# Samples' delta rule on TensorE: states streamed past w and q, and state updates on two row groups

## The chip, the cores and the metric

The kernel runs on one core of one Trainium2 chip. The time is that of one whole execution on the device in microseconds (us), as the median of several runs. Engines: TensorE (PE; its weight loads are listed as PEld), VectorE (DVE), ScalarE (ACT), GpSimd (POOL), and SyncE (SP), which issues most DMAs.

## The reference

A decoder trunk of two layers takes one step for a prompt of 512 tokens and for 8 samples of 8 new tokens each. In each layer one input projection feeds three mixers in parallel: a linear recurrence (RG-LRU), sparse attention (NSA), and the gated delta rule. Their outputs are gated, projected, merged and added to the residual. All is float32.

The change concerns the delta rule of the samples. It has 4 heads and, for each sample b and head h, a state S of 128x128. With a chunk's u, w, q, k (after decay), the reference's step is

```python
def step(S, xs):
    u_, w_, qk_, qdec_, kdec_, gl_ = xs
    vn = u_ - jnp.einsum('bhcd,bhde->bhce', w_, S)
    o = jnp.einsum('bhcd,bhde->bhce', qdec_, S) + jnp.einsum('bhce,bhef->bhcf', qk_, vn)
    S = gl_[..., None, None] * S + jnp.einsum('bhcd,bhce->bhde', kdec_, vn)
    return S, o
```

For the samples one chunk holds a sample's 8 tokens, so each of the 32 states is multiplied with 8 rows of w and 8 of q, and updated once. Outputs are o (normed and gated further on) and the new states.

## The kernel before

Activations lie channels on partitions, tokens along the free axis: 576 tokens (512 + 64), in halves of 288. All work is written out once per layer for each engine; each engine runs its own list in order, and counting semaphores join them.

**The dense stream.** TensorE's projections are cut into units (UNITS), each of 4 or 8 dense steps; a step is one matmul of 128x128 stationary with 288 columns (mm at L935), in the trace two records. A unit goes to PSUM bank u % 2 and is evicted by DVE or ACT; TensorE waits, before unit u, for the eviction of unit u-2. Two chunks of channels form a pair of seven units, named "1", "6", "2", "7", "5", "4", "3" in this order (PRODUCTS), of 4 steps each: a product scheme with sums of activations and of weights. Units "1" and "2" are evicted by ACT, the others by DVE. At the eviction of a "5", DVE also forms the three weight sums of the next pair (weight_sums: three operations on 128x512, L1804, L1801, L1804), for which it first waits until that pair's slot of the weight ring has landed; at that of a "6" it forms a fourth. The ring has two slots (RING). From L1226 on the order of pairs is: the last pair of z gates of the delta rule, then the merge gates ("mg") of branch 0, where each pair is followed by four units "ow" (output projection) of 4 steps. ACT turns the gates of "5", "4" and "3" of a merge pair into tanh when it comes to the unit two further on.

**What sets the order.** Between TensorE's small steps stand fills: fill(n, end) issues the next n dense steps, up to unit `end`. Each small step calls step(name), which records how many dense units were complete at that place. take_before(name, count), in DVE's and ACT's lists, evicts all the units recorded there before the engine waits for that step. So the count of dense steps ahead of a small step decides which evictions stand ahead of its consumer. The fills here end at unit U_MG2 at the latest (in attention 7 units later).

**The delta rule of the samples** (last entry of DN_GROUPS), by TensorE's lines:
- L1216/L1217: u and w, turned, to banks 6 and 7 (f_mm). The fill of 4 steps behind it is unit "5" of the last z pair. DVE copies uT (L2165), ACT wT (L1670).
- L1226, 32 matmuls: the state S0[:, b, h] is stationary (128x128), 16 columns stream past it, 8 of w and 8 of q of one sample. Step b_pe 1. DVE subtracts (L2168, helper line L1804), b_vt.
- turns of vn (helper line L864), b_pe 2; DVE copies vn (L2172), b_vn; L1239, products within the chunk, b_pe 3; DVE adds to q (L2178, L2179), b_so. ACT, which waits for b_so, squares it (L1688).
- for each head h, L1248: two matmuls of 512 columns, 64 tokens contracted. The moving operand bvm is vn of this head repeated 8 times under a mask of samples (bmask), made by DVE (L2186, helper line L1798, 64x1024), b_vm. Steps b_pe 4 to 7. DVE adds the result (two banks, 128x1024) to the states (L2193, helper line L1801), b_sn. Before each add, DVE takes the evictions recorded at that head's step.
- POOL decays the states in place (L824) behind b_pe 1, four operations.

After the loop TensorE waits for the fourth b_sn, then fills 2 steps and goes on with the sums of squares (L968, on column groups of 32, for the norms "o", "k", "q") and six broadcasts of the roots (L981, on row groups of 32), each followed by a product on DVE (L1981); then the keys are turned (L864). ACT waits for the fourth b_sn too, and forms logarithms (L1575), roots (L1582) and SiLU (L1706).

**SP's list.** After weights(19), the slot of merge pair 0, SP waits for the fourth b_vm (L684), then issues two loads of constants (L685: 858 KB, L686: 576 KB, into places that the delta rule used till then) and only then weights(20), the slot of merge pair 1 (L619, 1024 KB).

The end of DVE's loop over the heads (from L2181 on):

```python
                for h in range(DN_H + 1):
                    ...
                    if h >= 1:
                        g = h - 1
                        dve.wait_ge(s["b_gl"], past["b_gl"] + h)
                        take_before("b_pe", 3 + h)
                        dve.wait_ge(s["b_pe"], past["b_pe"] + 3 + h)
                        ...
```

## Time and profile before

| | |
|---|---|
| median of 3 runs | 1883.47 us (1881.01 to 1885.6) |
| the profiled execution | span 1882.8 us; no other time of it is given |
| TensorE busy | 1816.3 us, 96% |
| VectorE, ScalarE, GpSimd busy | 964.6, 516.7, 91.5 us |
| mean granted TensorE clock | 0.994 |
| DMA | 170.08 MB, mean 90 GB/s |

In a row of the timeline or of the chain the first number is the start in us from the span's start, the second the length in us; then come engine, line, operation, tiles, shapes and the number of records (x). A float32 matmul has two records. Square brackets give the time that the engine stood idle before it, and what ended that. DVE's operations are made by helpers, so that L1798 is any multiply, L1801 any add, L1804 any subtract, and L864 any turn; the shape tells which one it is. The granted clock is a share of 2.4 GHz.

### The profile page before, as it was taken

What the parts mean: (1) busy time and instruction counts of PE and PEld (TensorE: products, weight loads), DVE (VectorE), ACT (ScalarE), POOL (GpSimd) and SP (SyncE); (2) the same over time, 40 slices, a digit from 0 to 9 for tenths busy, and PEclk for the clock granted to TensorE, in tenths of its full rate; (3) what the DMA queues carried; (4) which work ended last, traced back from release to release, by engine and by line L of the source; (5) the groups of instructions that cost most, each with busy time, mean ns of one, the idle gap of its engine ahead of it and who ended that gap; (6) DMA issues with size and microseconds to landing.
All of it is one profiled execution on the core that took longest, in us unless ns stands there. A gap on an engine that the chain in (4) does not pass through costs nothing.

```text
span 1882.8 us, 29564 instructions
## 1 busy us (share of the span) xinstructions
PE 1816.3 (96%) x11454; PEld 1301.3 (69%) x11454; DVE 964.6 (51%) x2246; ACT 516.7 (27%) x1161; POOL 91.5 (5%) x133
## 2 busy tenths in 40 slices
PE   7999999999899999999999999999999999999999
PEld 5777688886665577676467777888856555776763
DVE  2749554534765555533137585545347565554321
ACT  3142313013356612200112433020142565221100
POOL 0000201001200000000000002010012000000000
PEclk9999999998999999999999999999999999999999
DMA  6312402023341135645042142021144311464411
GB/s 214 97 46 70 113 26 45 24 62 102 114 134 34 31 110 159 182 138 161 0 161 83 52 100 62 24 46 55 31 132 130 88 34 34 133 190 127 157 73 39
DMA packets 196529, 170.08 MB, mean 90 GB/s; under 512 B 49248, under 2 KB 186898, under 8 KB 195942
## 3 DMA queue, kind: packets, MB, share of 16 engines
q1 hardware_dynamic: 192164, 150.11, 27.4%
q0 software_dynamic: 4064, 18.03, 3.0%
q8 instruction: 91, 1.49, 0.3%
q14 instruction: 48, 0.39, 0.1%
q10 hardware_dynamic: 162, 0.05, 0.0%
HBM read 153.67 MB, written 21.71 MB: 93 GB/s over the span
## 4 chain that ended last, share of the span: by engine, by line
PE 81%; DVE 11%; issue 3%; SPq 2%; ACT 2%; DMA 1%; ACTq 0%; DVEq 0%
PE PS L935 53%; PE PS L864 6%; DVE arena L1873 3%; PE PS L1307 2%; PE PS L1320 2%; PE PS L1155 2%; PE PS L1137 1%; PE PS L1157 1%; DVE arena L1798 1%; PE PS L1376 1%; SPq L652 1%; PE PS L1226 1%; PE PS L1041 1%; PE PS L1248 1%; PE PS L1169 1%
## 5 line engine op out<-in xcount | busy, mean ns | idle before, releaser
L935 PE MATMUL PS<-hT,ring 128*128 128x288 f32 x2464 | 655.1, 411 | 7.5 <-DVE arena L2082 3.7
L935 PEld LDWEIGHTS PS<-hT,ring 128*128 128x128 f32 x2464 | 456.3, 191 | 138.7 <-issue 11.7
L935 PE MATMUL PS<-tt,ws 128*128 128x288 f32 x736 | 207.3, 414 | 13.4 <-DVE sg L1931 4.4
L935 PE MATMUL PS<-zs,owr 128*128 128x288 f32 x768 | 208.3, 413 | 6.8 <-DVE sg L1804 4.2
L935 PEld LDWEIGHTS PS<-zs,owr 128*128 128x128 f32 x768 | 140.0, 192 | 50.3 <-issue 12.8
L935 PEld LDWEIGHTS PS<-tt,ws 128*128 128x128 f32 x736 | 132.7, 190 | 57.6 <-issue 9.4
L864 PE MATMUL PS<-con,arena 128*128 128x128 f32 (+5 forms) x934 | 144.6, 281 | 14.4 <-DMA arena<-in_nsa_k_norm 10.3
L864 PEld LDWEIGHTS PS<-con,arena 128*128 128x128 f32 (+5 forms) x934 | 107.7, 140 | 72.8 <-issue 42.2
L1801 DVE TENSOR_TENSOR sg<-PS,sg 128x288 f32<-128x288 f32 x140 | 64.0, 457 | 139.7 <-PE PS L935 138.4
L935 PE MATMUL PS<-arena 128*128 128x512 f32 (+1 forms) x320 | 124.8, 594 | 2.1 <-DVE sg L1931 2.1
L935 PE MATMUL PS<-tt,ring 128*128 128x288 f32 x368 | 107.5, 426 | 0.0
L1873 DVE SCALAR_TENSOR_TENSOR arena<-arena,par 128x512 f32<-128x512 f32 x192 | 99.4, 518 | 6.3
L935 PEld LDWEIGHTS PS<-arena 128*128 128x128 f32 (+1 forms) x320 | 52.8, 180 | 71.0 <-issue 68.0
L1557 ACT ACTIVATE sg<-PS 128x288 f32<-128x288 f32 x46 | 18.5, 403 | 260.1 <-PE PS L935 259.9
L1731 ACT ACTIVATE arena<-PS,sm 128x128 f32<-128x128 f32 (+3 forms) x128 | 66.8, 523 | 70.8 <-DVE sm L2282 64.9
L935 PEld LDWEIGHTS PS<-tt,ring 128*128 128x128 f32 x368 | 69.1, 197 | 20.9 <-issue 3.0
L2282 DVE CUSTOM_DVE_ANT_0 PS<-PS,con 128x128 f32<-128x128 f32 (+3 forms) x128 | 61.8, 505 | 41.1 <-PE PS L1307 41.1
L1804 DVE TENSOR_TENSOR arena<-arena,PS 128x512 f32<-128x512 f32 (+3 forms) x70 | 43.4, 622 | 56.0 <-PE PS L1157 36.7
L1722 ACT ACTIVATE arena<-arena,sm 128x128 f32<-128x128 f32 (+3 forms) x128 | 64.7, 553 | 23.3 <-DVE sm L1798 23.3
L1798 DVE TENSOR_TENSOR arena<-arena 128x2304 f32<-128x2304 f32 (+3 forms) x24 | 39.7, 1655 | 58.1 <-ACT arena L1612 22.2
L1962 DVE SCALAR_TENSOR_TENSOR arena<-PS,arena 128x512 f32<-128x512 f32 x18 | 12.5, 692 | 103.9 <-PE PS L935 97.2
L1804 DVE TENSOR_TENSOR ws<-ring 128x512 f32<-128x512 f32 x92 | 63.5, 690 | 3.3 <-DMA ring<-in_w_in 1.7
(306 smaller groups left out, 2123.6 us busy)
## 6 DMA issues: line engine op xcount, KB each, us to landing
ring<-in_w_in SPq DMA_DIRECT2D x54, 1024.0 KB, 5.4
arena<-in_cache_nsa_kv SPq DMA_DIRECT2D x128, 192.0 KB, 2.7
ring<-in_w_in SPq DMA_DIRECT2D x32, 256.0 KB, 4.6
arena<-in_state_nsa_win SPq DMA_DIRECT2D x32, 256.0 KB, 3.4
arena<-in_cache_nsa_kv SPq DMA_DIRECT2D x128, 64.0 KB, 1.8
arena<-in_w_out SPq DMA_DIRECT2D x4, 2048.0 KB, 8.3
out_win_sample<-in_state_nsa_win POOLq DMA_DIRECT2D x2, 4032.0 KB, 23.1
arena<-in_x_prompt SPq DMA_DIRECT2D x8, 512.0 KB, 5.5
```

Source lines behind the costliest of these rows:

```text
L864: return nc.tensor.transpose(dst, src, ident[0:src.shape[0], 0:src.shape[0]])
L935: ins = mm(to, w, x, start=start, stop=stop, skip_group_check=True)
L1155: mm(new[0][m], Y[m, h, m], blocks(w[m], sz, 0), start=True, stop=True)
L1307: mm(PS[:, 4 + g, 0:q0 + P], qk7[m, r, q0:q0 + P], qk7[m, 5 + br, 0:q0 + P], start=True, stop=True).then_inc(s["a_s"], 1)
L1320: ins = mm(PS[g * HD:(g + 1) * HD, 7, rp * 2 * P:(rp + 1) * 2 * P], ktok[:, kb, col:col + HD], pTring[j % 2][:, g * 2 * P:(g + 1) * 2 * P] ...
L1722: A(p, p, ACT.Copy, scale=sm8[:, 7, u % 8:u % 8 + 1]).then_inc(s["a_n"], 1)
L1731: A(pring[slot % PRING][:, 0:width], PS[:, 4 + slot % 2, 0:width], ACT.Exp, scale=-1.0, bias=sm8[:, 0, k:k + 1], accum_out=sm8[:, 1, k:k + ...
L1798: return V.tensor_tensor(dst, a, b, ALU.mult)
L1801: return V.tensor_tensor(dst, a, b, ALU.add)
L1804: return V.tensor_tensor(dst, a, b, ALU.subtract)
L1873: ins = stt(out=d, in0=e, scalar=w(j), in1=d, op0=ALU.mult, op1=ALU.add)
L2282: V.tensor_tensor_reduce(out=raw, in0=raw, in1=C("causal")[:, 3 * P - q0:4 * P], scale=-1.0, scalar=-NEG, op0=ALU.add, op1=ALU.min, accum_ ...
```

## The change

The states become the moving operand. For each head and each pair j of samples, 32 stationary columns (8 of w and 8 of q of both samples) stand in column group j, and the two states of the pair stream past them, 256 columns; each sample's own rows come out token-first, with the other sample's beside them, unused. ACT and DVE copy the two result banks to SBUF (swq), eight turns bring them back channels-first in banks 6 and 7, and DVE takes from these the w part (two subtractions) and the q part (two copies). A fill of 6 steps stands between the products and the turns. DVE lays q beside w first (f_v 5). Between w products and vn's turns there is thus one b_pe step more. The state update of each head contracts 32 tokens (4 samples) on each of two row groups, with a mask of 4 columns, so that bvm is 64x512 instead of 64x1024, and each of the two matmuls gives four samples.

```diff
@@ -69,7 +69,7 @@
-    ("U", P), ("R", P), ("Um", P), ("Us", P), ("Rs", P), ("Ums", P), ("lev", 7 * P), ("bmask", DEC_BATCH),
+    ("U", P), ("R", P), ("Um", P), ("Us", P), ("Rs", P), ("Ums", P), ("lev", 7 * P), ("bmask", DEC_BATCH // 2),
@@ -124,7 +124,7 @@
-    c["bmask"] = np.arange(DEC_BATCH)[None, :] == row // DEC_SEQ
+    c["bmask"] = np.arange(DEC_BATCH // 2)[None, :] == row // DEC_SEQ % (DEC_BATCH // 2)
@@ -333,8 +333,8 @@
-    i_wm=31, i_x=31, i_xm=31, f_mm=5, f_u=4, f_v=4, f_w=5, m_mm=3, u_mm=4, f_m=3, q_w=3, q_s=4, q_n=3, q_oe=4, b_gl=4,
-    b_pe=7, b_so=1, b_vt=1, b_vn=1, b_vm=4, b_sn=4, dn_ok=1, mg_ok=32, small_in=96, sm_in=32, ln_ok=5, sum_ok=97,
+    i_wm=31, i_x=31, i_xm=31, f_mm=5, f_u=4, f_v=6, f_w=6, m_mm=3, u_mm=4, f_m=3, q_w=3, q_s=4, q_n=3, q_oe=4, b_gl=4,
+    b_pe=8, b_so=1, b_vt=1, b_vn=1, b_vm=4, b_sn=4, dn_ok=1, mg_ok=32, small_in=96, sm_in=32, ln_ok=5, sum_ok=97,
@@ -468,16 +468,28 @@
         uT, vnT = (arena[:, at + k * DN_H * T_S:at + (k + 1) * DN_H * T_S].rearrange("p (h n) -> p h n", h=DN_H)
                    for k in range(2))
         vn = tmp["B"][0:T_S, 1]
-        wT0, dc0 = A_DN["Sb"][0], A_DN["c"][0]
-        wT = arena[:, wT0:wT0 + DN_H * T_S].rearrange("p (h n) -> p h n", h=DN_H)
-        def w_and_q(h, b):
-
-            a, q = wT0 + h * T_S + b * DEC_SEQ, dc0 + h * T + SEQ + b * DEC_SEQ
-            return arena[:, a:a + 2 * (q - a)].rearrange("p (x c) -> p x c", x=2)[:, :, 0:DEC_SEQ]
+        wq = area(A_DN, "Sb").rearrange("p (h j x u) -> p h j x u", h=DN_H, j=4, x=2)
+        def w_and_q(h, j):
+            return area(A_DN, "Sb")[:, (4 * h + j) * 32:(4 * h + j) * 32 + 32]
+        def by_pairs(ap):
+            return ap.rearrange("p h (j u) -> p h j u", j=4)
         S0 = area(A_DN, "S0").rearrange("p (b h e) -> p b h e", b=DEC_BATCH, h=DN_H)
         rowd = area(A_DN, "rowd")[0:27]
-        bvm = [area(A_DN, "kbv")[:, k * 1024:(k + 1) * 1024] for k in range(2)]
+        bvm = [area(A_DN, "kbv")[:, k * 512:(k + 1) * 512] for k in range(2)]
+        swq = area(A_DN, "kbv")[:, 1024:2048]
+        def from_state(i, x):
+            return PS[:, 6 + i, :].rearrange("p (h j x u) -> p h j x u", h=DN_H, j=4, x=2)[:, :, :, x, i * DEC_SEQ:(i + 1) * DEC_SEQ]
+        def of_pairs(ap, i):
+            return ap.rearrange("p h (j i t) -> p h j i t", i=2, t=DEC_SEQ)[:, :, :, i]
         def diagonal(n):
@@ -1220,11 +1232,20 @@
                         fill(4, u0 + U_MG2)
                         pe.wait_ge(s["f_w"], past["f_w"] + k + 1)
                         pe.wait_ge(s["s0_in"], past["s0_in"] + 16 * DEC_BATCH)
+                        pe.wait_ge(s["f_v"], past["f_v"] + 5)
                         for h in range(DN_H):
-                            for b in range(DEC_BATCH):
-                                at = h * P + b * 2 * DEC_SEQ
-                                ins = mm(PS[:, 3, at:at + 2 * DEC_SEQ].rearrange("p (x t) -> p x t", x=2), S0[:, b, h, :],
-                                         w_and_q(h, b), start=True, stop=False, skip_group_check=True)
+                            for j in range(4):
+                                dst = PS[32 * j:32 * j + 32, 4 + h // 2, h % 2 * 2 * P:(h % 2 + 1) * 2 * P]
+                                ins = mm(dst.rearrange("p (i e) -> p i e", i=2), w_and_q(h, j), S0[:, 2 * j:2 * j + 2, h, :],
+                                         start=True, stop=True, skip_group_check=True)
+                        step("b_pe")
+                        ins.then_inc(s["b_pe"], 1)
+                        fill(6, u0 + U_MG2)
+                        pe.wait_ge(s["f_w"], past["f_w"] + 6)
+                        pe.wait_ge(s["f_v"], past["f_v"] + 6)
+                        for i in range(2):
+                            for h in range(DN_H):
+                                ins = turn(PS[:, 6 + i, h * P:(h + 1) * P], swq[:, (2 * h + i) * P:(2 * h + i + 1) * P])
                         step("b_pe")
                         ins.then_inc(s["b_pe"], 1)
                         fill(4, u0 + U_MG2)
@@ -1245,8 +1266,8 @@
-                                ins = mm(PS[:, 4 + 2 * (h % 2) + c, :], kq[0:T_S, 0, h, 0:P],
-                                         bvm[h % 2][0:T_S, c * 512:(c + 1) * 512], start=True, stop=True)
+                                m = slice(32 * c, 32 * c + 32)
+                                ins = mm(PS[:, 4 + 2 * (h % 2) + c, :], kq[m, 0, h, 0:P], bvm[h % 2][m], start=True, stop=True)
@@ -1667,8 +1688,11 @@
                     if TILES[group[0]][0] >= SEQ:
                         take_before("f_mm", NTILE)
                         act.wait_ge(s["f_mm"], past["f_mm"] + NTILE)
-                        A(wT, bank4(7, T_S), ACT.Copy).then_inc(s["f_w"], 1)
-                        take_before("b_pe", 3)
+                        A(wq[:, :, :, 0], by_pairs(bank4(7, T_S)), ACT.Copy).then_inc(s["f_w"], 1)
+                        take_before("b_pe", 1)
+                        act.wait_ge(s["b_pe"], past["b_pe"] + 1)
+                        A(swq[:, 0:512], PS[:, 4, :], ACT.Copy).then_inc(s["f_w"], 1)
+                        take_before("b_pe", 4)
                         act.wait_ge(s["b_so"], past["b_so"] + 1)
                         break
                     for li, k in enumerate(group):
@@ -1686,7 +1710,7 @@
                 for n in range(DN_H):
                     A(dc[:, 4 + n], dc[:, n], ACT.Square).then_inc(s["sq_ok"], 1)
-                take_before("b_pe", 3 + DN_H)
+                take_before("b_pe", 4 + DN_H)
                 act.wait_ge(s["pv"], taken(u0 + U_NZ, "V"))
                 act.wait_ge(s["pa"], taken(u0 + U_NZ, "A"))
                 act.wait_ge(s["b_sn"], past["b_sn"] + DN_H)
@@ -2162,34 +2186,39 @@
                 take_before("f_mm", NTILE)
                 dve.wait_ge(s["f_mm"], past["f_mm"] + NTILE)
+                V.tensor_copy(wq[:, :, :, 1], by_pairs(dc[:, 0:4, SEQ:T])).then_inc(s["f_v"], 1)
                 link(V.tensor_copy(uT, bank4(6, T_S)))
                 take_before("b_pe", 1)
                 dve.wait_ge(s["b_pe"], past["b_pe"] + 1)
-                sub(vnT.rearrange("p h (b t) -> p h b t", t=DEC_SEQ), uT.rearrange("p h (b t) -> p h b t", t=DEC_SEQ),
-                    PS[:, 3, :].rearrange("p (h b x t) -> p h b x t", h=DN_H, x=2, t=DEC_SEQ)[:, :, :, 0]).then_inc(s["b_vt"], 1)
+                V.tensor_copy(swq[:, 512:1024], PS[:, 5, :]).then_inc(s["f_v"], 1)
                 take_before("b_pe", 2)
                 dve.wait_ge(s["b_pe"], past["b_pe"] + 2)
-                V.tensor_copy(vn, bank4(2, P, T_S)).then_inc(s["b_vn"], 1)
+                q_s = dc[:, 0:4, SEQ:T]
+                for i in range(2):
+                    ins = sub(of_pairs(vnT, i), of_pairs(uT, i), from_state(i, 0))
+                ins.then_inc(s["b_vt"], 1)
+                for i in range(2):
+                    ins = V.tensor_copy(of_pairs(q_s, i), from_state(i, 1))
+                link(ins)
                 take_before("b_pe", 3)
                 dve.wait_ge(s["b_pe"], past["b_pe"] + 3)
-                from_s = PS[:, 3, :].rearrange("p (h b x t) -> p h b x t", h=DN_H, x=2, t=DEC_SEQ)[:, :, :, 1]
-                within = PS[:, 2, 0:DN_H * T_S].rearrange("p (h b t) -> p h b t", h=DN_H, t=DEC_SEQ)
-                q_s = dc[:, 0:4, SEQ:T].rearrange("p h (b t) -> p h b t", t=DEC_SEQ)
-                link(V.tensor_copy(q_s, from_s))
-                add(q_s, q_s, within).then_inc(s["b_so"], 1)
+                V.tensor_copy(vn, bank4(2, P, T_S)).then_inc(s["b_vn"], 1)
+                take_before("b_pe", 4)
+                dve.wait_ge(s["b_pe"], past["b_pe"] + 4)
+                add(q_s, q_s, PS[:, 2, 0:DN_H * T_S].rearrange("p (h n) -> p h n", h=DN_H)).then_inc(s["b_so"], 1)
                 dve.wait_ge(s["b_vn"], past["b_vn"] + 1)
                 for h in range(DN_H + 1):
                     if h < DN_H:
                         if h >= 2:
-                            take_before("b_pe", 3 + h - 1)
-                            dve.wait_ge(s["b_pe"], past["b_pe"] + 3 + h - 1)
-                        mul(bvm[h % 2][0:T_S].rearrange("p (b e) -> p b e", b=DEC_BATCH),
-                            rep(vn[:, h, :], DEC_BATCH), bc(C("bmask")[0:T_S], P)).then_inc(s["b_vm"], 1)
+                            take_before("b_pe", 4 + h - 1)
+                            dve.wait_ge(s["b_pe"], past["b_pe"] + 4 + h - 1)
+                        mul(bvm[h % 2][0:T_S].rearrange("p (b e) -> p b e", b=DEC_BATCH // 2),
+                            rep(vn[:, h, :], DEC_BATCH // 2), bc(C("bmask")[0:T_S], P)).then_inc(s["b_vm"], 1)
                     if h >= 1:
                         g = h - 1
                         dve.wait_ge(s["b_gl"], past["b_gl"] + h)
-                        take_before("b_pe", 3 + h)
-                        dve.wait_ge(s["b_pe"], past["b_pe"] + 3 + h)
+                        take_before("b_pe", 4 + h)
+                        dve.wait_ge(s["b_pe"], past["b_pe"] + 4 + h)
                         add(S0[:, :, g], S0[:, :, g],
                             PS[:, 4 + 2 * (g % 2):6 + 2 * (g % 2), :].rearrange("p a (b e) -> p (a b) e", e=P))\
                             .then_inc(s["b_sn"], 1)
```

## Rows read from the trace of the kernel before

**Rows 1.** The page, part 4: shares of the chain that ended last.

```profile
PE 81%; DVE 11%; issue 3%; SPq 2%; ACT 2%; DMA 1%; ACTq 0%; DVEq 0%
```

**Rows 2.** The chain in order of time, layer 0: start, us, what.

```profile
282.87 1.94 PE PS L935 x8
...
424.40 9.28 PE PS L1226 x64
433.68 4.03 PE PS L935 x8
...
440.84 1.03 PE PS L1239 x8
...
444.01 1.94 PE PS L1248 x4
...
448.09 1.91 PE PS L1248 x4
450.00 2.14 PE PS L935 x8
...
461.20 1.11 PE PS L968 x16
```

**Rows 3.** The same chain, layer 1.

```profile
1355.46 8.57 PE PS L1226 x64
1364.03 3.84 PE PS L935 x8
1367.87 0.44 PE PS L864 x4
...
1379.40 2.14 PE PS L935 x8
```

**Rows 4.** Busy time by stretch; the number behind POOL is the granted clock.

```profile
433.40:437.00 3.60, 3.60 (x9) 2.62 (x9) 0.42 (x1) 0.00 (x0) 3.16 (x2) 0.50 0.00 0
```

**Rows 5.** Timeline of DVE, POOL and SP, layer 0.

```profile
433.84 7.51 POOL L824 TENSOR_TENSOR arena<-arena 128x1024 f32<-128x1024 f32 x4 [35.57 <-PE PS L1226]
...
451.17 1.21 DVE L1798 TENSOR_TENSOR arena<-arena,con 64x1024 f32<-64x1024 f32 x1
...
452.41 0.34 SPq L685 DMA_DIRECT2D con<-in_con  x1
...
458.13 1.22 DVE L1801 TENSOR_TENSOR arena<-arena,PS 128x1024 f32<-128x1024 f32 x1 [1.40 <-PE PS L1248]
...
461.35 0.69 DVE L1804 TENSOR_TENSOR ws<-ring 128x512 f32<-128x512 f32 x1 [0.62 <-DMA ring<-in_w_in]
```

**Rows 6.** Timeline of DVE, layer 1.

```profile
1380.58 1.21 DVE L1798 TENSOR_TENSOR arena<-arena,con 64x1024 f32<-64x1024 f32 x1
...
1387.54 1.22 DVE L1801 TENSOR_TENSOR arena<-arena,PS 128x1024 f32<-128x1024 f32 x1 [1.39 <-PE PS L1248]
...
1391.18 0.69 DVE L1804 TENSOR_TENSOR ws<-ring 128x512 f32<-128x512 f32 x1 [1.05 <-DMA ring<-in_w_in]
```

**Rows 7.** The chain in order of time, three other stretches.

```profile
10.83 1.97 PE PS L864 x8
...
20.65 0.87 PE PS L864 x8
...
475.30 0.70 PE PS L981 x8
```

**Rows 8.** Timeline of ACT and PE in the norms, layer 0.

```profile
466.36 1.28 ACT L1537 ACT_TABLE_LOAD   x1
...
479.60 0.41 ACT L1557 ACTIVATE sg<-PS 128x288 f32<-128x288 f32 x1
...
484.56 1.72 PE L935 MATMUL PS<-hT,ring 128*128 128x288 f32 x6
...
491.13 1.24 PE L935 MATMUL PS<-tt,ws 128*128 128x288 f32 x4 [1.52 <-DVE arena L1981]
...
502.60 0.88 PE L864 MATMUL PS<-con,arena 128*128 128x128 f32 x6 [0.63 <-DVE arena L1801]
```

## Prediction

> **What bounds the kernel now.** I read the chain of waits first: TensorE holds 81% of it, VectorE 11% [rows 1]. So time comes off only where TensorE's own order gets shorter, and goes back on wherever that order meets a wait. Then I read the chain in order of time through the samples' delta rule, which is TensorE's stretch from the state products (L1226) to the fourth state update (L1248) [rows 2, 3]. The reader is to see that TensorE never stands still there: between the small steps lie fills of four dense steps each (8 records, 1.94 us undisturbed, 2.14 us beside a small step [rows 2]). The state products alone take 9.28 us in the first layer and 8.57 in the second [rows 2, 3], and behind them the granted clock is 0.50 [rows 4], 1.2 instead of 2.4 GHz, so that the next fill takes 4.03 and 3.84 us instead of 2.14 [rows 2, 3]. Last I read what DVE and SP do beside it, because the change shifts TensorE's order against theirs [rows 5, 6].
>
> **The parts, on TensorE, from the start of L1226 to the end of the second state update.** Before: 450.00 - 424.40 = 25.60 us in layer 0, 1379.40 - 1355.46 = 23.94 in layer 1 [rows 2, 3].
>
> State products. 64 records with 16 columns moving become 32 with 256 moving, on four column groups. L968 has this form: 16 records of 288 columns on four groups took 1.11 us [rows 2]. One after another they would take 16 x 1.94/8 = 3.9, so the groups run side by side. I take 2 x 1.11 x 256/288 = 1.97 us; if the groups ran singly it were 32 x 0.2425 x 256/288 = 6.90, and these are the two bounds. I take the lower, since L968 differs only in what is streamed. The Trainium skill (TensorE: Matmul & The Clock Gate, "Part 3: Packing small matmuls — row/col tiling") gives 2.38 times for three column tiles, which is less than side by side; scaled to four it is 3.17 times and the term 2.2 us, an estimate. The row shows 3.5 times.
>
> Fill of six steps, new: 1.5 x 1.94 = 2.91. It is dense work pulled forward, so it comes back as a lead of six steps. Eight turns, new: 0.87 us for eight [rows 7], with a change of form some 0.95. Fill 2.14, turns of v 0.44 as in layer 1 [rows 3], fill 1.94, within-chunk products 1.03 [rows 2]: the clock's loss is gone, since whole streams replace sixteen columns. Fill 2.14.
>
> State updates. Four records of 512 columns (1.94, 1.91) [rows 2] become two pairs on two row groups. L981 has the form on four: 8 records of 288 columns in 0.70 instead of 1.94 [rows 7]. So 1.91/2 and 0.1 of overhead: 1.06; bounds 0.95 and 1.91. Twice, with a fill of 2.14 between: 4.26.
>
> Sum after: 1.97 + 2.91 + 0.95 + 2.14 + 0.44 + 1.94 + 1.03 + 2.14 + 4.26 = 17.78. The second update ends 7.8 us sooner in layer 0 (at 442.2) and 6.2 in layer 1 (at 1373.2).
>
> Edits at no cost. DVE's copy of q and uT, and ACT's of w, lie under the fill that follows f_mm. The two copies of the state products, on ACT and DVE, lie under the fill of six: DVE first evicts a dense unit and forms three weight sums, and is still done before those 2.9 us end. The two subtractions instead of one lie under the next fill. POOL's decay of the states starts behind the first b_pe as before and takes 7.5 us [rows 5]; the first add comes some 13 us behind it. Without those fills each copy would cost its own length, 0.4 to 0.7 us. DVE's mask multiply halves from 1.21 to about 0.66 [rows 5].
>
> **The wait that is new.** This is the term that decides. DVE evicts dense units up to each b_pe step before it goes on. Dense steps since f_mm: before, the fourth update (b_pe 7) stands at 28 steps, that is seven units, after "7" of merge pair 0. With six more it stands at 34, and unit "5" (emitted at 32) is now in front of it. Evicting a "5" brings the three weight sums of the next slot, and these wait for that slot's load. SP starts this load only after the fourth mask multiply and two loads of constants. Before, the multiply ended at 451.17 + 1.21 = 452.38, SP issued from 452.41, and DVE, held by the DMA, began the sums at 461.35 [rows 5]: 8.97 us later; in layer 1 1381.79 to 1391.18, 9.39 [rows 6]. The kernel before had the last add of the states (458.13 + 1.22 = 459.35 [rows 5]; 1388.76 [rows 6]) ahead of the sums. The changed one has it behind them, and TensorE waits for this add before its next fill; ACT and POOL wait for it too.
>
> After, layer 0: multiply done at 442.2 + (452.38 - 450.00) - 0.55 = 444.0; load landed 453.0; sums 3 x 0.67 (one is 0.69 long [rows 5], they overlap slightly) 455.0; add 456.2. Layer 1: 1373.2 + 1.85 = 1375.05; 1384.4; 1386.4; 1387.65. TensorE would be there at 442.2 + 2.14 + 1.06 + 2.14 + 1.06 + 2.05 = 450.65 and 1381.65: it stands still 5.6 and 6.0 us. The last add comes 3.15 and 1.1 us sooner than before, and six dense steps (2.9 us) further on in each layer: 4.25 + 5.8 = 10.1 us.
>
> **What is given back.** The norms follow, in layer 0 counted from the last add (459.35 before). First ACT. It turns to the tanh of merge pair 0 before each dense unit it takes; before, two of them fell together between two logarithms, with one table load of 1.28 us there [rows 8] and one back. Six steps further on the three fall before three different logarithms: the first finds its table loaded, the others each need two loads, so 4 instead of 2, 2.55 us more. So its copy of the next "1" (479.60, 20.25 us after the add [rows 8]) comes at 22.8. TensorE needs it for the "2" of merge pair 1, at dense step 304 (counted from the first of the q units; f_mm stands at 240): from step 278 that is 26 steps x 0.485 + 3 x 1.11 + 2 x 0.70 = 17.3 us, so it waits 5 us and goes on at 23.2. Before, it came there at 484.56, 25.2 us behind the add, but with four of the six broadcasts done [rows 8]; after, with two. Four more at 3 steps and 0.7 us each end at 31.9. Then DVE has an eviction and three sums (2.5 us from the last broadcast's start, 31.2) ahead of the last product (1.4): 35.1, where before it was 491.13, at 31.8 [rows 8]. Up to the turns of the keys DVE then sets the pace, 11.45 us before (502.60 [rows 8]), of which the three sums, now done, were 2.0: 44.55 after, 43.25 before. So 1.3 us of each lead of 2.9 is lost. At the end of attention the dense budget ends six steps sooner, where TensorE is nearly full without it: 0.5. Together 2 x 1.8 = 3.6; the bounds are nothing and the whole lead, 5.8.
>
> Sum: 1882.8 - 10.1 + 3.6 = 1876.3 on the profiled span. The median of the runs lies 0.7 above that span: 1877.0.
>
> **Rivals.**
> (a) The wait at the fourth update doesn't arise, because the load lands sooner. Then the add follows the update 1.2 us on, at 449.85 and 1380.85, 13.1 us sooner in all; but DVE meets the load just behind it, and TensorE waits about 3 us per layer for the next eviction: 1877.0 - 13.1 + 6 = 1869.9. For it: DMA is otherwise idle. Against: 8.97 and 9.39 us agree. Chance 0.11.
> (b) The clock falls in the new pause. The first eight turns, after the pause that opens the kernel, took 1.97 us, the same later 0.87 [rows 7], although the row of those us shows no lower clock; the price of a fall here is what followed the state products, 4.03 - 2.14 = 1.9 us, or twice that. TensorE has the 5 us by which it waits for ACT to spare right after the pause, which hides most; if it hides nothing, 2 x 1.9: 1880.8. Chance 0.18. The Trainium skill (same page, "Why this matters for your kernels") asks that no long idle gaps stand between bursts of products, or the clock drops to half; by that rule this happens in both layers.
> (c) Slower: column and row groups run one after another, L1226's successor taking 6.9 us and the updates 1.9. That is 4.9 + 1.7 us per layer ahead of the load: 1877.0 + 13.2 = 1890.2. It decides from 4.9 us per layer on. L968 and L981 speak against it; for it only that the streams come from a strided area of states. Chance 0.03.
>
> Forecast case 0.64 (its own range 1872.5 to 1881.5); 0.04 is left for what I don't see. 0.2% is 3.8 us, about what a measurement of this kernel can tell: same is 1879.7 to 1887.2. Faster: 0.64 x 0.86 + 0.11 + 0.18 x 0.35 = 0.72; same 0.22; slower 0.06. The range takes (a)'s neighbourhood and (b): 1868 to 1883.
>
> **What would show it.** Right: some 2 us of L1226's successor, no granted clock of 0.50 behind it, updates of 1.06 us, the last 1024-element add behind three weight sums released by the ring's load, and a pause of TensorE of about 6 us before L968 in each layer. Wrong: that add right behind the fourth update (a); a low clock after the pause with all later steps later (b); a state step of 7 us (c); or new waits of more than 3 us per layer in the norms.

## The result, and the profile after

The changed kernel is slower: 1902.96 us median of 4 runs (1899.64 to 1906.58) against 1882.24 (1879.65 to 1885.6), a ratio of 1.0099 with an interval of 1.0083 to 1.0115. The forecast was 1877.0 with a range of 1868 to 1883. The profiled span is 1901.8 us.

The page of the changed kernel, parts 1 and 4:

```profile
span 1901.8 us, 29481 instructions
...
PE 1805.0 (95%) x11406; PEld 1286.5 (68%) x11406; DVE 961.0 (51%) x2254; ACT 524.8 (28%) x1167; POOL 92.2 (5%) x133
...
PE 76%; DVE 11%; issue 3%; ACT 3%; SPq 3%; DMA 2%; ACTq 0%; DVEq 0%
```

In the chain that ended last TensorE has fallen from 81% [rows 1] to 76%; ScalarE, SP's queue and the DMAs have one point more each. In the new listing dense steps are L947 (L935 before), turns L876 (L864), state products L1239 (L1226), within-chunk products L1260 (L1239), state updates L1270 (L1248), sums of squares L980 (L968).

The chain in order of time, layer 0, changed kernel (start, us, what), beside [rows 2]:

```profile
424.45 1.86 PE PS L1239 x32
426.31 3.11 PE PS L947 x12
429.42 0.87 PE PS L876 x8
...
434.61 1.03 PE PS L1260 x8
...
440.98 1.08 PE PS L1270 x4
...
444.85 8.10 DMA ring<-in_w_in
452.97 0.69 DVE ws L1828
...
454.91 1.23 DVE arena L1825
456.18 2.29 PE PS L947 x4
458.46 1.83 PE PS L980 x16
```

The stage came out as worked out beforehand. The state products take 1.86 us instead of 9.28, the second update 1.08, and it ends at 442.06. Then the chain leaves TensorE for the load of the ring and the last state add. TensorE goes on at 456.18 with its first sum of squares at 458.46, against 461.20 before [rows 2]: 2.7 us sooner, with six dense steps more behind it.

All of the loss comes later. TensorE's waits in the whole trace (us in total, times, longest), first the changed kernel:

```profile
PE PS L947 <- DVE arena L1825: 12.0, 4, 6.0
...
PE PS L947 <- DMA owr<-in_w_lru_out: 9.0, 2, 4.7
...
PE PS L947 <- DVE arena L2005: 6.1, 2, 3.1
PE PS L1341 <- DVE zs L1822: 5.8, 2, 2.9
PE PS L947 <- ACT sg L1578: 5.6, 2, 2.8
PE PS L947 <- DMA owr<-in_w_dn_out: 3.8, 2, 2.6
```

and the kernel before:

```profile
...
PE PS L935 <- DVE sg L1804: 4.2, 2, 2.1
...
PE PS L935 <- DVE arena L1981: 3.1, 2, 1.5
PE PS L1320 <- DVE zs L1798: 3.0, 2, 1.5
PE PS L935 <- DMA owr<-in_w_dn_out: 2.6, 2, 1.5
```

Before, TensorE waited neither for output weights of the LRU branch (w_lru_out) nor for ScalarE's copy of a unit "1" (L1578). One wait has gone: the 4.2 us for the evictions that stood behind the weight sums. The timeline of TensorE in the changed kernel, layer 0 (start, us, instruction, and in brackets how long it had stood still and what released it), shows them in place:

```profile
456.18 2.29 PE L947 MATMUL PS<-hT,ring 128*128 128x288 f32 x4 [5.62 <-DVE arena L1825]
...
479.89 2.91 PE L947 MATMUL PS<-hT,ring 128*128 128x288 f32 x6 [2.80 <-ACT sg L1578]
...
494.09 3.80 PE L947 MATMUL PS<-tt,ring 128*128 128x288 f32 x8 [3.06 <-DVE arena L2005]
...
505.01 0.88 PE L876 MATMUL PS<-con,arena 128*128 128x128 f32 x6 [1.31 <-DVE arena L1825]
...
537.55 0.72 PE L947 MATMUL PS<-zs,owr 128*128 128x288 f32 x2 [4.66 <-DMA owr<-in_w_lru_out]
...
639.71 0.65 PE L1341 MATMUL PS<-arena 128*64 128x256 f32 x4 [2.88 <-DVE zs L1822]
...
787.11 1.91 PE L947 MATMUL PS<-zs,owr 128*128 128x288 f32 x4 [2.64 <-DMA owr<-in_w_dn_out]
```

Behind these waits of layer 0 the clock is low. Busy time by stretch, changed kernel; the number behind POOL's is the granted clock:

```profile
424.40:441.00 16.60, 16.60 (x103) 11.57 (x102) 9.82 (x19) 3.82 (x7) 7.80 (x4) 1.00 0.00 0
...
453.00:457.00 4.00, 0.82 (x2) 0.68 (x3) 3.45 (x5) 0.76 (x2) 0.57 (x1) 0.50 0.00 0
...
480.30:483.70 3.40, 3.40 (x12) 1.76 (x10) 2.01 (x3) 0.00 (x0) 0.00 (x0) 0.50 0.00 0
...
494.00:497.30 3.30, 3.21 (x7) 2.36 (x8) 2.59 (x2) 0.00 (x0) 1.98 (x4) 0.50 0.32 50
...
538.30:541.70 3.40, 3.40 (x12) 1.99 (x13) 0.94 (x6) 1.84 (x7) 0.00 (x0) 0.50 0.98 308
640.80:644.00 3.20, 3.20 (x10) 1.87 (x8) 0.35 (x3) 2.06 (x5) 0.00 (x0) 0.50 0.00 0
787.60:790.80 3.20, 3.20 (x10) 2.28 (x10) 0.00 (x0) 0.90 (x2) 0.00 (x0) 0.50 0.22 63
```

Through the whole new stage the clock is at its full level (1.00, 2.4 GHz), where it was 0.50 behind the state products [rows 4] (and, in the kernel before, already from 429.2 to 433.6, in their second half). But it is 0.50, that is 1.2 GHz, in or behind each pause of the timeline above that is longer than 2 us: 5.62, 2.80, 3.06, 4.66, 2.88 and 2.64 us. Over the span the mean granted clock is 0.989, and 0.994 before. The low clock removed behind the state products has come back at other places, and more of it.

Not every such pause has a low clock with it. In layer 1 it is 0.50 in or behind the pauses of 5.97, 4.31 and 2.88 us, but two that are as long as in layer 0 have 1.00 behind them, and the dense steps run at full speed:

```profile
1424.05 1.72 PE L947 MATMUL PS<-hT,ring 128*128 128x288 f32 x6 [2.80 <-ACT sg L1578]
...
1437.51 2.21 PE L947 MATMUL PS<-tt,ring 128*128 128x288 f32 x8 [3.06 <-DVE arena L2005]
```

The state products of layer 1 start at 1367.95 instead of 1355.46 [rows 3]: layer 0 alone has lost 12.5 us, although it was ahead at its last state add.

### The profile page after: what moved, and what is told of

The parts are those of the page before. It is cut to its first block, busy times and chain, and to the rows that moved or that the text cites. A ratio compares the mean times of both kernels' runs of the same rounds, so it can differ in the third digit from the quotient of the medians.

```text
span 1901.8 us, 29481 instructions
## 1 busy us (share of the span) xinstructions
PE 1805.0 (95%) x11406; PEld 1286.5 (68%) x11406; DVE 961.0 (51%) x2254; ACT 524.8 (28%) x1167; POOL 92.2 (5%) x133
## 4 chain that ended last, share of the span: by engine, by line
PE 76%; DVE 11%; issue 3%; ACT 3%; SPq 3%; DMA 2%; ACTq 0%; DVEq 0%
PE PS L947 50%; PE PS L876 5%; DVE arena L1897 3%; PE PS L1328 2%; PE PS L1341 2%; SPq L664 2%; PE PS L1167 1%; PE PS L1149 1%; SPq L671 1%; PE PS L1169 1%; PE PS L1397 1%; DVE arena L1822 1%; DMA ring<-in_w_in 1%; PE PS L1053 1%; DVE arena L1825 1%
## 5 line engine op out<-in xcount | busy, mean ns | idle before, releaser
L947 PE MATMUL PS<-hT,ring 128*128 128x288 f32 x2464 | 657.3, 411 | 24.3 <-DVE arena L1825 12.0
L947 PEld LDWEIGHTS PS<-hT,ring 128*128 128x128 f32 x2464 | 456.1, 191 | 155.5 <-DVE arena L1825 13.8
L947 PE MATMUL PS<-zs,owr 128*128 128x288 f32 x768 | 210.1, 417 | 12.8 <-DMA owr<-in_w_lru_out 9.0
L947 PE MATMUL PS<-tt,ws 128*128 128x288 f32 x736 | 206.9, 414 | 9.2 <-DVE sg L1955 4.4
L947 PEld LDWEIGHTS PS<-zs,owr 128*128 128x128 f32 x768 | 141.1, 193 | 60.1 <-issue 27.0
L947 PEld LDWEIGHTS PS<-tt,ws 128*128 128x128 f32 x736 | 132.6, 190 | 51.3 <-issue 8.6
L876 PE MATMUL PS<-con,arena 128*128 128x128 f32 (+5 forms) x950 | 146.6, 281 | 17.5 <-DMA arena<-in_nsa_k_norm 10.8
L876 PEld LDWEIGHTS PS<-con,arena 128*128 128x128 f32 (+5 forms) x950 | 109.8, 140 | 76.0 <-issue 43.1
L947 PE MATMUL PS<-arena 128*128 128x512 f32 (+1 forms) x320 | 124.8, 593 | 2.1 <-DVE sg L1955 2.1
L947 PE MATMUL PS<-tt,ring 128*128 128x288 f32 x368 | 107.7, 426 | 6.1 <-DVE arena L2005 6.1
L947 PEld LDWEIGHTS PS<-arena 128*128 128x128 f32 (+1 forms) x320 | 52.7, 179 | 71.1 <-issue 68.1
L1578 ACT ACTIVATE sg<-PS 128x288 f32<-128x288 f32 x46 | 18.6, 404 | 275.2 <-PE PS L947 275.2
L947 PEld LDWEIGHTS PS<-tt,ring 128*128 128x128 f32 x368 | 69.4, 197 | 28.4 <-DVE arena L2005 7.0
L1828 DVE TENSOR_TENSOR ws<-ring 128x512 f32<-128x512 f32 x92 | 63.4, 689 | 14.1 <-DMA ring<-in_w_in 12.4
L1558 ACT ACTIVATE sg<-sg 128x288 f32<-128x288 f32 x72 | 31.4, 436 | 132.3 <-DVE sg L1825 104.3
L1828 DVE TENSOR_TENSOR arena<-arena,PS 128x512 f32<-128x512 f32 (+3 forms) x72 | 43.4, 608 | 45.9 <-PE PS L1169 36.7
```

The source lines that it names most:

```text
L876: return nc.tensor.transpose(dst, src, ident[0:src.shape[0], 0:src.shape[0]])
L947: ins = mm(to, w, x, start=start, stop=stop, skip_group_check=True)
L1828: return V.tensor_tensor(dst, a, b, ALU.subtract)
```

## The experiments

Times were taken beside runs of the kernel before on the same chip: 1884.65 us median for the first four, 1884.47 for the next four, 1883.35 for the last three. The intervals of the ratios are 2 to 5 us wide to each side, so a difference of a few us between two of these runs is not resolved. My theory after the result: what costs is the lead. The change puts six more dense steps ahead of the last state add and of all that comes from it. Dense steps then come before their inputs (weights held by SP's order, copies of ScalarE, scaled q of VectorE), TensorE stands still, and behind many of these pauses the clock is low. The rival: the new forms or the added short steps cost by themselves.

**Aligned: the change without its lead.** In this order behind the state products, the turns and the turns of v:

```diff
-                        fill(6, u0 + U_MG2)
+                        fill(4, u0 + U_MG2)
...
-                        fill(4, u0 + U_MG2)
+                        fill(2, u0 + U_MG2)
...
-                        fill(4, u0 + U_MG2)
+                        fill(2, u0 + U_MG2)
```

> The changed kernel with fills of 4, 2 and 2 steps behind the state products, the eight turns and vn's turns, instead of 6, 4 and 4: the dense stream then stands at every state update exactly where it stood before. Theory L (the six dense steps pulled forward did the harm: they put the weight sums and their load ahead of the last add, and what followed is their doing): the last add comes behind the fourth update again, no pause over 3 us in the norms, and what the new products and updates save on TensorE, 12.4 + 10.8 us by the chain, arrives: 1861 us, 1857 to 1868. Rival C (the new form itself costs it, because the stage now ends before the load of the next slot, or the copies and turns stand in the way): the pauses only move, 1885 to 1903.

Measured: 1860.76 us (1858.31 to 1861.88), ratio 0.9867 (0.9846 to 0.9887), mean clock 0.998. The sizes of three fills are worth 42 us, and every new form is still in. The first sum of squares starts at 449.00, where it was 461.20 [rows 2] and, in the changed kernel, 458.46. The timeline of VectorE in this kernel shows why the late load does no harm here:

```profile
445.94 1.22 DVE L1825 TENSOR_TENSOR arena<-arena,PS 128x1024 f32<-128x1024 f32 x1 [0.55 <-PE PS L1270]
...
451.52 0.69 DVE L1828 TENSOR_TENSOR ws<-ring 128x512 f32<-128x512 f32 x1 [2.99 <-DMA ring<-in_w_in]
```

The last add is ahead of the weight sum that waits for the load; in the changed kernel it is behind.

**The load of merge pair 1 first.** The changed kernel, SP's list:

```diff
+                weights(l * NS + 20)
                 sp.wait_ge(s["b_vm"], past["b_vm"] + DN_H)
...
-                weights(l * NS + 20)
```

> The changed kernel with SP issuing the load of merge pair 1's slot before it waits for the fourth mask multiply, not behind the two loads of constants; fills untouched, so the six-step lead stays. Theory L in its first part (the sums wait for a load that SP holds back): the pauses of 5.6 and 6.0 us before the sums of squares vanish, the three sums (2.0 us) still stand ahead of the last add and cost at most 0.5 us of pause, and the later waits (ACT's tables, projection weights behind the cached keys) stay: 1903 - 12 - up to 4 of low clock = 1889, 1884 to 1893. Rival (the load wasn't what held DVE, or its bandwidth is the limit and the wait only moves to the constants): 1898 to 1904.

Measured: 1889.4 us (1886.93 to 1893.25), ratio 1.0022 (1.001 to 1.0034). The pause at the last add is gone and 13.6 us with it: the two pauses were 5.62 and 5.97, 11.6 together. Whether they cost more than their own length this run doesn't show: the 2 us between lie inside the intervals of the two ratios, and the profiled spans differ by 12.0 (1901.8 and 1889.8). The other waits stay:

```profile
PE PS L947 <- DMA owr<-in_w_lru_out: 8.7, 2, 4.5
...
PE PS L947 <- DVE arena L2005: 6.1, 2, 3.1
PE PS L1341 <- DVE zs L1822: 5.8, 2, 2.9
PE PS L947 <- ACT sg L1578: 5.6, 2, 2.8
```

**The lead alone, in the kernel before.**

```diff
-                        fill(4, u0 + U_MG2)
+                        fill(10, u0 + U_MG2)
                         pe.wait_ge(s["b_vt"], past["b_vt"] + 1)
```

> The kernel before with a fill of 10 steps instead of 4 behind its state products: the lead of six steps alone, none of the new code. Theory L: the fourth b_sn waits behind the three sums here as well (pause of about 4.5 us per layer), the same tables, the same wait for projection weights, low clock behind the pauses: 1882 + 30 to 42 = 1918, 1905 to 1926. Rival C: dense work moved forward costs nothing, 1880 to 1886.

Measured: 1923.48 us (1922.5 to 1925.24), ratio 1.0205 (1.0184 to 1.0226). Six dense steps moved forward, none added, nothing else touched: 39 us slower, and with the waits of the changed kernel, by the names of the old lines:

```profile
PE PS L935 <- DVE arena L1801: 9.9, 4, 5.0
PE PS L935 <- DMA owr<-in_w_lru_out: 8.6, 2, 5.0
...
PE PS L935 <- DVE arena L1981: 6.1, 2, 3.1
PE PS L1320 <- DVE zs L1798: 5.8, 2, 2.9
```

This run settles it that the loss isn't in the new forms.

**Half the lead.** The changed kernel with fill(3) instead of fill(6) behind the state products.

> The changed kernel with 3 steps instead of 6 between the state products and the eight turns: a lead of three. Theory L: unit 5 of merge pair 0 ends one step behind the fourth update (31 against 32 steps), so the add goes ahead of the sums; one more pair of table loads on ACT than before (2.6 us, partly hidden) and half of the later wait for projection weights: 1862 + 3 to 10 = 1868, 1862 to 1875. If the harm grows evenly with the lead: halfway between the aligned kernel and the changed one, about 1882. Rival C: no gain beyond 1.5 us, 1899 to 1903.

Measured: 1874.87 us (1871.54 to 1879.42), ratio 0.9955 (0.9931 to 0.9979), at the upper edge of what was expected. With three steps the wait for ScalarE's copy is gone and that for w_lru_out is down to 1.6 us in all, but another has grown, TensorE's for VectorE's eviction at L1953, from 1.1 us in the aligned kernel to 8.4:

```profile
PE PS L947 <- DVE arena L1953: 8.4, 2, 4.4
```

VectorE itself had stood still for 8.17 us there, until ScalarE's tanh (L1558) was done, so this is ScalarE's list again. Three steps cost 14 us against the aligned kernel and six cost 42: the cost doesn't grow evenly with the lead, and the waits listed are not the same ones.

**Aligned, with the load first.** Both edits above.

> The aligned version (fills 4, 2, 2) with the load of merge pair 1 issued ahead of SP's wait for the fourth mask product. In the aligned run VectorE's weight sum waited 2.99 us for that load, but behind the last state add, and no wait of TensorE came out of it. Theory L (a late load costs only where a dense step that waits for it stands ahead of work that TensorE's short products wait for): no difference to the aligned run, 1861 (1858 to 1864). Rival (the load is worth what it was worth under the lead, 13.6 us of 1903, or its 3 us per layer): 1847 to 1856.

Measured: 1861.33 us (1858.08 to 1864.28), ratio 0.9871 (0.9849 to 0.9893): no difference to the aligned run. The same edit that was worth 13.6 us under the lead is worth nothing without it.

**Aligned, without the row groups.** The mask and bvm are for eight samples again, and

```diff
-                                m = slice(32 * c, 32 * c + 32)
-                                ins = mm(PS[:, 4 + 2 * (h % 2) + c, :], kq[m, 0, h, 0:P], bvm[h % 2][m], start=True, stop=True)
+                                ins = mm(PS[:, 4 + 2 * (h % 2) + c, :], kq[0:T_S, 0, h, 0:P],
+                                         bvm[h % 2][0:T_S, c * 512:(c + 1) * 512], start=True, stop=True)
```

> The aligned version without the second part of the change: the state update has one row group again (bvm 1024 columns wide, a mask product of all eight samples, two products of 512 columns on all 64 tokens). Theory (the row groups are worth the difference of two such products, 1.94 to 1.08 us, four times in each layer, and nothing else): 6.9 us slower than the aligned run, 1867.7 (1864 to 1872). Rival (VectorE's mask product, 1.21 instead of 0.66 us, sets the distance of the updates, or the row groups are hidden behind it): 1861 to 1863 if hidden, 1872 to 1880 if VectorE becomes the bound.

Measured: 1865.5 us (1864.63 to 1866.19), ratio 0.9896 (0.9879 to 0.9912): 4.7 us slower than the aligned run, between the theory's 6.9 and the rival's 0 to 2. The updates are back at 1.98 and 1.91 us, and the first one of layer 0 waits 0.57 us for VectorE's mask product. The first sum of squares of layer 1 starts at 1374.48 instead of 1367.64, 6.8 us later: up to there the theory holds. Behind that point some of it comes back, for the profiled spans differ by only 2.8 us (1862.7 and 1859.9): the aligned run has two stretches of 3.4 us at a clock of 0.50 there (around 1411 and 1442), this one none before 1850. Such stretches come and go between these two runs, and they are as large as what was to be measured.

**The row groups alone, in the kernel before.**

> The kernel before with the row groups of the state update alone; the products of the states and every fill as before. Nothing is put ahead of the last state add that was not there. Theory L (the row groups are sound and keep the order of the work): 6.9 us faster than before, 1877.7 (1874 to 1881) against 1884.65. Rival (part of the loss of the changed kernel lies in the row groups, by a pause or a fall of the clock): 1884 or slower.

Measured: 1877.61 us (1872.37 to 1884.75), ratio 0.9958 (0.994 to 0.9976). Sound by themselves, and worth 6.9 us there, as 8 x (1.94 - 1.06) = 7.0 has it.

**Two loads earlier, the lead kept.** Beside the load first, in SP's list:

```diff
+                out_weights(l * NO + 4)
+                out_weights(l * NO + 5)
                 cached_keys(0)
                 window_keys(0)
-                out_weights(l * NO + 4)
-                out_weights(l * NO + 5)
```

The reason is in SP's timeline of the changed kernel, layer 0 (start, us, instruction):

```profile
515.55 17.50 SPq L671 DMA_DIRECT2D arena<-in_cache_nsa_kv  x16
533.09 0.44 SPq L679 DMA_DIRECT2D arena<-in_state_nsa_win  x1
533.58 1.05 SPq L647 DMA_DIRECT2D owr<-in_w_lru_out  x2
```

SP issues the weights of output units 4 and 5 behind sixteen transfers of cached keys, at 533.58, while TensorE stands at 532.9 waiting for them. In the kernel before SP issued the same weights 3.2 us sooner, and TensorE came to them only at 536.39:

```profile
530.38 1.05 SPq L635 DMA_DIRECT2D owr<-in_w_lru_out  x2
```

> The changed kernel with the load of merge pair 1 issued first, as in the run before (1889.4), and with SP issuing the weights of output units 4 and 5 ahead of the sixteen transfers of cached keys instead of behind them. Theory L (each pause behind the lead is a dense step that came before what it needs, here weights held by SP's own order): the wait for them, 8.7 us in two layers, goes, with the low clock behind it (two stretches of 3.4 us at half speed, 3.4 us): 1877.5 (1874 to 1883). Rival (the pause moves on to the next thing that is late, since the lead is still there): 1886 to 1890.

Measured: 1877.74 us (1874.83 to 1879.78), ratio 0.9959 (0.9944 to 0.9974), 11.7 us less than with the load first alone. The wait for w_lru_out is gone from the list, and the three waits shown below it for the run with the load first stand there unchanged: 6.1, 5.8 and 5.6 us. A little has moved on, as the rival has it: the wait for the cached keys (L1407) is 2.9 us instead of 1.2. So of the 42 us between changed and aligned kernel, 13.6 hang on the first load and 11.7 on the second; the 17 left over I put down to these three waits and smaller ones.

**The lead given back before the last add.** The changed kernel, its 6, 4 and 4 kept, and in the state updates

```diff
-                            fill(4, u0 + U_MG2)
+                            fill(4 if h == 3 else 2, u0 + U_MG2)
```

> The changed kernel with its 6, 4 and 4 dense steps behind the products of the states and the turns, and 2 instead of 4 behind each of the first three state updates: six dense steps stand ahead of the turns that did not before, none more ahead of the last add. Theory L (what costs is the number of dense steps issued ahead of the last state add and of all that comes from it, not where among the short products they stand): like the aligned run, 1862 (1859 to 1867), and no wait of over 3 us for the load of merge pair 1. Rival (the six behind the products of the states cost in themselves, whether or not the lead is taken back): 1875 to 1903.

Measured: 1860.85 us (1859.45 to 1864.11), ratio 0.9885 (0.986 to 0.9909). The six steps behind the state products cost nothing that these runs resolve. What counts is how many dense steps stand ahead of the last add and of what comes from it, not where among the short steps they are. One part of the expectation missed: VectorE's weight sum waited 4.49 us for the load of merge pair 1, more than the 3 expected. But the last add stood ahead of it, and TensorE's longest wait for an eviction behind these sums (sg, L1828) is 2.1 us, as in the aligned kernel.

**The lead given back in the norms.** The load first, and

```diff
-                fill(6, u0 + U_MG2)
+                fill(3, u0 + U_MG2)
                 square_sums(past, "q", "sum2", rs7[:, 0:4])
-                fill(8, u0 + U_MG2)
+                fill(5, u0 + U_MG2)
```

> The changed kernel with the load of merge pair 1 issued first (1889.4), and with three dense steps fewer ahead of the sums of squares of q and three fewer behind them: the lead of six is still there at the last add and is gone at the broadcasts of the norms. Theory L (of the 28 us between that run and the aligned one, nearly all arises behind the sums: ScalarE's copy, the scaled q, the output weights, the first products of attention): 1867 (1861 to 1876), with the waits for the output weights, the scaled q and ScalarE's copy back at those of the aligned run, and the wait of the sums for ScalarE, 3.2 us, kept or longer. Rival (the loss arises at the add and the sums, and the later waits only pass it on): 1880 to 1890.

Measured: 1869.45 us (1866.46 to 1872.41), ratio 0.9931 (0.9904 to 0.9957). 20 of the 28 us are gone with the waits behind the sums. So the larger part of the harm arises behind the last add, which still has its lead of six here. What is left is for the most part the wait of the sums of q for ScalarE's logarithm, grown as expected from 3.2 to 6.1 us:

```profile
PE PS L980 <- ACT arena L1596: 6.1, 2, 3.0
```

**A lead of minus two.** The aligned kernel with the load first, and fills 3 and 1 instead of 4 and 2 behind state products and turns.

> The aligned version with the load first (1861.3) and with one dense step fewer behind the products of the states and one fewer behind the turns (3 and 1): a lead of minus two. Theory L (a lead costs because dense steps come before their inputs; without one nothing is left to win by it, and a smaller cover for the copies and the subtraction may open a pause of up to 0.5 us in each layer): 1861 (1859 to 1864). Rival (the cost goes on falling with the lead, as from six steps to three and from three to none): 1853 to 1857.

Measured: 1867.36 us (1866.05 to 1867.91), ratio 0.9915 (0.9893 to 0.9937). Both expectations missed; it is 6 us slower. The waits that opened are on the short steps' side:

```profile
PE PS L993 <- DVE arena L2005: 8.1, 4, 3.9
PE PS L876 <- DVE arena L1825: 6.9, 2, 3.4
```

Those are the broadcasts of the norms and the turns of the keys. With fewer dense steps in front of them TensorE comes to them before the norms' chain on ScalarE and VectorE is through. The cover for the copies, which I had watched, was not what ran out (the first update of layer 0 waits 0.72 us for the mask product, but that is small beside them). So the lead can be too large and too small: six steps more cost 42 us, three more 14, two fewer 6.

The best version is the aligned one: 24 us faster than the kernel before, 42 faster than the changed one. The lead given back in the updates equals it.

## Why the prediction was wrong

**State products, turns, updates: right.** The sum was 17.78 us for the part, and it is 442.06 - 424.45 = 17.61 in layer 0. The products took 1.86 us (1.97 forecast, 6.90 one after another, which is 3.7 times), the turns 0.87 (0.95), the updates 1.06 and 1.08 (1.06). Rival (c) falls. The Trainium skill (TensorE: Matmul & The Clock Gate, "Part 3: Packing small matmuls — row/col tiling") gives 2.38 times for three column tiles. The estimate scaled from it to four was 2.2 us; the trace has 1.86 us, and the trace decides.

**Edits at no cost: right.** No wait of TensorE stands for a copy or subtraction in that stage.

**The wait that is new: right in place and size.** Last add 456.2 forecast, 456.12 measured; pauses 5.6 and 6.0 forecast, 5.62 and 5.97 measured. Rival (a) didn't come.

**What is given back: wrong.** It was priced at 3.6 us, with the bounds "nothing and the whole lead, 5.8". In the norms of layer 0 it held at first: the copy of ScalarE let TensorE go on at 479.89 (479.4 by the forecast). But the last q product came at 494.09, 38.0 us behind the add where 35.1 was forecast, and the keys' turns at 48.9 instead of 44.55. Two stretches of 3.4 us at half speed, behind 480.3 and 494.0, can make up to 3.4 us of these 4.3. Layer 1 says less: behind the same two pauses its clock was 1.00, and its keys' turns still came 47.1 us behind the add (1447.06 against 1399.97). By this comparison 1.8 us are the low clock; where the other 2.5 come from stays open.

The larger miss is the sentence "At the end of attention the dense budget ends six steps sooner ...: 0.5". From the keys' turns to the end of layer 0 the kernel went from 2.4 us behind (505.01 against 502.60) to 12.5 behind, and the lead of 2.9 us that should have come back there didn't: 13.0 us. The waits that the trace lists for this stretch come to 27.0 us, and to 19.3 before (7.7 more: 4.7 for w_lru_out, 1.5 more for w_dn_out, 1.4 more for L1341's input and smaller ones, less what fell away). Three stretches of 3.4 us at half the clock, behind the pauses of 4.66, 2.88 and 2.64, make 5.1 us more: 12.8 together.

Over the whole kernel, from the last add of each layer to the next layer's state products or to the end, the changed kernel took 15.7 us longer in layer 0 (1367.95 - 456.12 against 1355.46 - 459.35) and 7.8 in layer 1 (1901.8 - 1399.97 against 1882.8 - 1388.76). With the 2.9 us of lead that were already done, 18.6 and 10.7 us were given back, 29.3 in all, where the forecast had 1.8 each and 3.6 in all. This term is the step of the prediction that failed.

I had followed the lead on ScalarE and VectorE as far as the keys' turns, and not on SP. The output units 4 and 5 are dense work that comes sooner with the lead, while their load is tied by SP's order to the qk_ok step, a short step that came later. The rule that I used for the last add, what is late next, had to be used once more for each load behind it. And the bound was false in kind. A lead can cost more than its own length, because it isn't only lost: it opens pauses that were not there, and one lead opens several. In the kernel before, the same six steps alone, 2.9 us in each layer, cost 39 us.

**Rival (b), the clock falls in the new pause: it came, together with the forecast case, and not only there.** It was given 0.18 and 1880.8 us, for one pause per layer. "TensorE has the 5 us ... to spare" was right for that pause: four records and sixteen of the sums took 2.29 and 1.83 us behind it, against 1.07 (half of 2.14) and 1.11 before [rows 2], 1.9 us as priced, and the wait for ScalarE was 2.80 us instead of 5. What wasn't priced is the fall behind each of the pauses that follow. The Trainium skill (TensorE: Matmul & The Clock Gate, "Why this matters for your kernels") warns that the clock drops to half after long idle gaps between bursts. The rows agree in part: it happened at gaps of 2.64 to 5.97 us, and not at gaps of 2.80 and 3.06 in layer 1. Going by the mean granted clock, the shortfall from full is 0.011 x 1901.8, about 21 us of the span, and was 0.006 x 1882.8, about 11, before; in the aligned kernel it is 0.002 x 1859.9, about 4. The clock thus seems to have a good part in both differences; how much of the time it took is not separated by a run, as no run keeps the pauses and not the clock.

**The sign.** Without its lead the change is worth 24 us, against 10.1 - 3.6 = 6.5 in the forecast: no add waits for the load, and nothing is given back. With the lead it loses 20.7.

## What to carry to other kernels

When a change shortens one strand of work that is woven by hand into another, count the steps of the second strand that stand ahead of each hand-over, and keep this count as it was; only then read the gain of the new forms. A step pulled forward needs its inputs sooner too: follow it on every queue to the end of the stage, the one that issues its loads included, and don't bound its cost by its own length. Where a late load stands behind a wait in a list of transfers, it matters only if a step that needs it is ahead of work that the critical engine wants: the same reordering was worth 13.6 us in one version and nothing in another.

## What I had not expected of the hardware

In layer 0 of the changed kernel pauses of TensorE of only 2.64 to 3.06 us had a granted clock of 0.50 behind them, in which dense steps ran at half speed: eight records took 3.80 us at 494.09, where a fill of eight records takes 2.14 [rows 2]. In layer 1 the pauses of 2.80 and 3.06 us had 1.00 behind them, and there the eight took 2.21. In the kernel before a stretch at 0.50 in layer 1 stood behind waits of only 2.08 and 0.63 us, with short work between them:

```profile
1430.14 1.24 PE L935 MATMUL PS<-zs,owr 128*128 128x288 f32 x4 [2.08 <-DVE sg L1804]
1432.01 1.22 PE L864 MATMUL PS<-con,arena 128*128 128x128 f32 x6 [0.63 <-DVE arena L1801]
```

Busy time behind them, with the granted clock behind POOL's:

```profile
1432.60:1435.60 3.00, 3.00 (x9) 2.29 (x9) 2.54 (x2) 1.14 (x2) 0.92 (x2) 0.50 0.04 11
```

The same two waits in layer 0 (2.08 and 0.63 us, before 502.60) had a clock of 1.00 behind them. So the length of a pause doesn't tell alone whether it falls, and a change that adds pauses has a part of its cost that differs between two layers of one run. Removing a pause of 5.62 and one of 5.97 us gave back 13.6 us against 11.6 of their own length, which by the intervals is no more than their length.
